# A two-layer encoder trunk on one core: suffix-sum subtractions ahead of head sums, first activations rounded ahead of the second weight slot, and the next layer's first x tiles transposed between the last banks

## The reference

```python
for layer in range(2):
    h = rms_norm(x, norm1_g[layer])
    proj = h @ w_in[layer]              # q, k, v of three mixers and the gate logits
    ya = diff_attention(...)            # two softmax maps a head, partial rotary on q and k
    yb = chunk_band_attention(...)
    yc = stick_breaking_attention(...)  # log_keep = log_sigmoid(-z) below the diagonal;
                                        # later = suffix sum of log_keep over the keys
                                        # a = exp(log_sigmoid(z) + later)
    x = x + (sum of sigmoid(gate_i) * (y_i @ P_i)) @ w_out[layer]
    h2 = rms_norm(x, norm2_g[layer])
    x = x + peer(h2, ...)               # 16384 experts, top-16 a head, weights u and v
```

## Time and profile before

| | |
|---|---|
| median of 3 runs | 2221.88 us (2221.85 to 2223.79) |
| the profiled execution, its own time | 2224.01 us |
| its span, first to last instruction | 2222.3 us |
| PE busy | 2184.6 us, 98% of the span |
| DVE busy | 1591.6 us, 72% |
| ACT busy | 1197.9 us, 54% |
| POOL busy | 570.6 us, 26% |
| mean granted clock of PE | 0.996 |

### The profile page before, as it was taken

How to read it: one execution, slowest core, us unless ns; L and a number is a source line. 1 busy time by engine, 2 the same in 40 slices (tenths; PEclk the granted TensorE clock), 3 DMA queues, 4 the chain that set the end, 5 groups by cost and what they waited for, 6 DMA issues and landing times.

```text
span 2222.3 us, 41570 instructions
## 1 busy us (share of the span) xinstructions
PE 2184.6 (98%) x14116; PEld 1968.4 (89%) x14116; DVE 1591.6 (72%) x2784; ACT 1197.9 (54%) x1936; POOL 570.6 (26%) x286
## 2 busy tenths in 40 slices
PE   8999999999999999999999999999999999999999
PEld 6789999999999988888877899999899999888887
DVE  5667858978897556666657678599788975566665
ACT  5755545478885343333367554454788854333332
POOL 1300006876662000000013000178666610000000
PEclk9999999999999999999999999999999999999999
DMA  6444554544444556566654445445444445556564
GB/s 223 143 142 137 178 187 144 180 161 150 146 149 146 188 186 191 193 192 190 197 187 147 139 147 194 157 160 184 153 151 147 147 152 188 189 190 194 196 193 152
DMA packets 103761, 377.24 MB, mean 170 GB/s; under 512 B 11760, under 2 KB 11760, under 8 KB 103152
## 3 DMA queue, kind: packets, MB, share of 16 engines
q1 hardware_dynamic: 102528, 371.24, 51.0%
q10 hardware_dynamic: 1136, 4.79, 0.6%
HBM read 374.94 MB, written 1.05 MB: 169 GB/s over the span
## 4 chain that ended last, share of the span: by engine, by line
PE 94%; DVE 3%; ACT 2%; issue 1%; DMA 0%; SPq 0%; ACTq 0%; DVEq 0%
PE ps L489 29%; PE ps L490 28%; PE ps L491 28%; PE ps L806 3%; PE ps L498 1%; DVE w_lo L1252 1%; PE ps L616 1%; PE ps L775 1%; ACT w_hi L924 1%; PE ps L577 0%; DMA raw<-in_stream 0%; PE ps L589 0%; PE ps L687 0%; DVE arena L1353 0%; ACT hot L1172 0%
## 5 line engine op out<-in xcount | busy, mean ns | idle before, releaser
L1107 ACT ACTIVATE w_hi<-raw 128x1024 fp32r<-128x1024 f32 x512 | 521.4, 1055 | 510.1 <-PE ps L491 509.9
L489 PE MATMUL ps<-hT_hi,w_hi 128*128 128x256 f32 x2688 | 770.5, 287 | 5.1 <-DVE arena L1670 5.1
L490 PE MATMUL ps<-hT_lo,w_hi 128*128 128x256 f32 x2688 | 762.6, 284 | 0.0
L491 PE MATMUL ps<-hT_hi,w_lo 128*128 128x256 f32 x2688 | 762.4, 284 | 0.0
L474 POOL TENSOR_TENSOR w_lo<-raw,w_hi 128x1024 fp32r<-128x1024 f32 x208 | 498.8, 2407 | 272.5 <-ACT w_hi L1107 272.5
L489 PEld LDWEIGHTS ps<-hT_hi,w_hi 128*128 128x128 f32 x2688 | 517.7, 193 | 10.6 <-issue 7.8
L490 PEld LDWEIGHTS ps<-hT_lo,w_hi 128*128 128x128 f32 x2688 | 517.9, 193 | 0.9
L491 PEld LDWEIGHTS ps<-hT_hi,w_lo 128*128 128x128 f32 x2688 | 517.5, 193 | 0.0
L1637 DVE TENSOR_TENSOR w_lo<-raw,w_hi 128x1024 fp32r<-128x1024 f32 x304 | 358.2, 1220 | 91.2 <-ACT w_hi L1107 91.2
L489 PE MATMUL ps<-w_hi,wgt_hi 128*128 128x512 f32 x1024 | 398.9, 390 | 0.5 <-DVE wgt_lo L1732 0.5
L490 PE MATMUL ps<-w_lo,wgt_hi 128*128 128x512 f32 x1024 | 398.6, 389 | 0.0
(11 more groups left out here) (194 smaller groups left out, 2515.5 us busy)
## 6 DMA issues: line engine op xcount, KB each, us to landing
raw<-in_w_u SPq DMA_DIRECT2D x256, 512.0 KB, 3.3
raw<-in_w_v SPq DMA_DIRECT2D x256, 512.0 KB, 3.8
raw<-in_stream SPq DMA_DIRECT2D x192, 512.0 KB, 3.3
arena<-in_bias ACTq DMA_DIRECT2D x2, 1024.0 KB, 5.8
arena<-in_subk ACTq DMA_DIRECT2D x2, 1024.0 KB, 6.4
x<-in_x SPq DMA_DIRECT2D x4, 256.0 KB, 5.6
out<-x SPq DMA_DIRECT2D x4, 256.0 KB, 2.0
arena<-in_params ACTq DMA_DIRECT2D x2, 283.5 KB, 6.3
```

What stands on the lines that cost most here:

```text
L489: mm(out_, left[0], right[0], start=start, stop=False, skip_group_check=group)
L490: mm(out_, left[0], right[1], start=False, stop=False, skip_group_check=group)
L491: return mm(out_, left[1], right[0], start=False, stop=stop, skip_group_check=group)
L1107: f(w_hi[:, slot, :], raw[:, slot, :], ACT.Copy).then_inc(hi_ready.sem, 1)
```

## The change

Four edits. On DVE, `c_take_later(0)` goes from after slot 22 to after slot 20 and `c_take_later(1)` from after slot 23 to after slot 21, and `head_block(2)` from after slot 20 to after slot 21, behind `c_take_later(1)`. On ACT, `round_tiles(0, (0, 1))` goes between `split(0)` and `split(1)`, and `load_small()` behind `split(1)`. On PE, tiles 0 and 1 of x are transposed before the layer loop (for layer 0) and after groups 1 and 2 of the last product (for the next layer; the loop does this in the last layer too); tile 2 stays at the head of the layer and tile 3 goes behind slot 0. On DVE, tiles 0 and 1 of the next layer are multiplied by the gain and their rests written between the last additions to x, and its slot 0 moves one addition ahead; the order of tiles 2 and 3 follows PE's.

```diff
+            norm_transposes(x_there, (0, 1))
             with pe.Fori(0, LAYERS) as layer:
...
-                norm_transposes(lambda n: pe.wait_ge(x_ready[n].sem, x_ready[n].at(layer, 16)), range(4))
+                norm_transposes(x_done, (2,))
...
+                        if 4 * cb + k == 0:
+                            norm_transposes(x_done, (3,))
...
                     last.then_inc((v_part if n < 3 else v_mm).sem, 1)
+                    if n in (1, 2):
+                        norm_transposes(x_next, (n - 1,))
...
+                split(0)
+                round_tiles(0, (0, 1))
+                split(1)
                 load_small()
-                split(0)
-                split(1)
-                round_tiles(0, (0, 1))
...
-                gain_tiles(0, (0, 1))
                 if layer == 0:
+                    gain_tiles(0, (0, 1))
                     split((0,))
-                rest_tiles(0, (0, 1))
+                    rest_tiles(0, (0, 1))
+                gain_tiles(0, (2,))
                 split((1,))
-                gain_tiles(0, (2, 3))
+                gain_tiles(0, (3,))
                 split((2,))
                 rest_tiles(0, (2, 3))
...
-                    19: ((c_sums, 1), (head_norm, 3)), 20: ((c_keep, 1), (head_block, 2)),
-                    22: ((c_take_later, 0), (head_norm, 4)), 23: ((c_take_later, 1), (head_norm, 5)),
+                    19: ((c_sums, 1), (head_norm, 3)), 20: ((c_keep, 1), (c_take_later, 0)),
+                    21: ((c_take_later, 1), (head_block, 2)), 22: ((head_norm, 4),), 23: ((head_norm, 5),),
...
-                    if n == 1 and layer + 1 < LAYERS:
-                        split((0,), layer + 1)
+                    if layer + 1 < LAYERS:
+                        if n == 0:
+                            split((0,), layer + 1)
+                        if n == 1:
+                            gain_tiles(0, (0,), layer + 1)
+                        if n == 2:
+                            rest_tiles(0, (0,), layer + 1)
+                            gain_tiles(0, (1,), layer + 1)
+                            rest_tiles(0, (1,), layer + 1)
```

More of the change, by code:

```diff
@@ L499, in transposes, with norm_transposes, x_there, x_done @@
                 return last
+            def norm_transposes(done, tiles):
+                for n in tiles:
+                    done(n)
+                    transposes(ps[:, n, :], x_tile(n), 4).then_inc(normT_mm.sem, 1)
+            def x_there(n):
+                pe.wait_ge(x_ready[n].sem, 16)
+            norm_transposes(x_there, (0, 1))
             with pe.Fori(0, LAYERS) as layer:
[L502 to L506, removed]
+                def x_done(n):
+                    pe.wait_ge(x_ready[n].sem, x_ready[n].at(layer, 16))
+                def x_next(n):
+                    pe.wait_ge(x_ready[n].sem, x_ready[n].at(layer, 32))
                 def spread(which):
@@ L1253, in split, with gain_tiles @@
                                         w_hi[:, i % SLOTS, :].bitcast(F), ALU.subtract).then_inc(w_ready.sem, 1)
-                def gain_tiles(which, tiles):
+                def gain_tiles(which, tiles, layer=layer):
                     for n in tiles:
@@ L1263, in gain_tiles, with rest_tiles @@
                                         gain.unsqueeze(2).broadcast_to([P, 4, P]), ALU.mult).then_inc(gained.sem, 1)
-                def rest_tiles(at, tiles):
+                def rest_tiles(at, tiles, layer=layer):
                     for n in tiles:
```

## The result

The changed kernel is slower: 2227.82 us, the median of 15 runs (2226.82 to 2230.05), against 2222.84 (2221.33 to 2227.07, 15 runs) for the kernel before, a ratio of 1.0021 with a 95% interval of 1.0014 to 1.0028. That is 5.0 us more, where the prediction had 0.9 less, and it is outside the range. The profiled execution has a span of 2226.4 us in place of 2222.3, so 4.1 us more to explain, and by page part 1 most of it is idle or slow time and not work: PE is busy for 2.5 us more, with eight more matmuls than before, which take 0.98 us at the pace of the earlier trace rows, and idle for 1.6 more.

The account below looks back on a forecast made before the run. PE, busy 98% of the span, was taken as the bound, with 9.0 us of waits as ceiling of direct gains. Terms -1.4 + 0 + 1.0 - 0.5 + 0 = -0.9 took 2221.88 to 2221.0 us, range 2216.8 to 2223.4.

Parts of the forecast that it names:

- the start of layer 1: From loop's turn to spread(0): slot 0 starts 1.35 us sooner, but the diagonal comes when it came; 0, bounds -0.7 to +0.5.
- The clock, term 0: Behind the suffix sums' idle: one slow matmul stretch in two layers, as before; 0 us, ends -1.6 and +1.6.
- Start of layer 0, -1.4: PE begins slot 0 at 10.45, takes the diagonal at 24.91 where spread(0) ran at 26.34: -1.4 us.
- The rests and the diagonal of layer 1: At layer 1's start the rests are ready, and PE waits up to 0.9 us for the diagonal before spread(0): 0.
- Last layer, +1.0: Two tiles' unused transposes between the last product's groups delay the last addition and store: +1.0 us, between 0.8 and 1.2.
- Suffix sums, -0.25 a layer: Piece 2's wait of 2.33 us becomes about 2.1 at piece 4: -0.25 us a layer, -0.5 in both.
- case 2: In the suffix sums POOL's powers aren't held and ACT is next: -1.06 us a layer, 2219.4 us; chance 0.15.
- case 5: In the suffix sums POOL's powers take longest, holding back piece 4: +2.2 a layer, 2225.9 us, 2227.5 with slow stretch; chance 0.04.

Follow-up runs that it names:

- The late wait alone: Kernel before plus one PE wait, ahead of group 3 of the last product, for the addition to x tile 1: 2227.44 us, ratio 1.0014.
- the loop written out: Changed kernel with PE's loop over the layers written out, nothing else changed: 2219.61 us, ratio 0.9982 to the kernel before.
- tile 0 alone ahead: Changed kernel with only tile 0 transposed between the last groups, tile 1 back at the layer's head: 2225.38 us, ratio 1.0011 to the kernel before.
- The suffix sums alone: Kernel before with only the change's new DVE order of the suffix sums: 2225.86 us, ratio 1.001.
- the start alone: Kernel before with only ACT's new order at the start and tile 3's transposes behind slot 0 in both layers: 2223.78 us, ratio 1.0001.
- the wait for tile 0: Kernel before plus one PE wait, ahead of group 3 of the last product, for the addition to x tile 0: 2221.98 us, ratio 0.9997.
- start and suffix sums: Changed kernel without its layer-boundary edit, so no transposes between the last groups: 2224.68 us, ratio 1.0006 to the kernel before.

## Why the prediction was wrong

**The failed step** as to the mechanism is in the start of layer 1; the clock, further down, is the other and costs more. It reads: "The loop's turn took 1.08 us from the last matmul's slot to 1117.66 and I see nothing that shortens it", with half a microsecond more as the upper bound. I took the idle time that the trace shows for the turn's cost. It was what stuck out from under the matmuls still queued. The change puts a wait on PE that ends at 1112.37 with one group behind it, and then 3.06 us stick out: 2.1 more. The late wait alone shows it (3.4 us, +1.7 to 2.4 at equal clock), and the loop written out shows the reverse (no idle time, 8.2 us less, though some 2 of them have nothing to do with the turn). With 2.1 more the prediction would have been 2223.1, still in its range; the clock took it out. The prediction asks what a step of DVE or POOL is queued behind, but didn't ask it of PE's own instruction stream at the new wait. The Trainium skill ("Perfetto Trace Analysis", section "Sequencer Loop") says that a sequencer pushes instructions for its engine into a queue and runs control instructions itself. The traces agree, in that the turn left 0.3 to 1.0 us idle where nothing held PE's instructions late, 1.5 with tile 0 alone ahead, and 3.1 to 3.5 where the wait for tile 1 did.

**The clock, term 0.** Its ends were -1.6 and +1.6, for one stretch. The profiled execution has three new ones at or behind places that bind (1117, 1209, 1803) and has lost one (96): two more, 3.2 us. The bound failed since it looked at one place only. Of the three, that at 1117 follows the idle time of the turn; that at 1803 can't be put down to the change. Idle of 2.2 us at piece 4, with eight transposes behind it, was priced as if it were the idle at piece 2. The suffix sums alone lower the mean clock as much as the whole change; why piece 4 is the worse place is not shown.

**Start of layer 0, -1.4:** right, -1.67 at the spread. Two misses in the working partly cancel: PE began 0.43 us sooner than predicted, and slot 0 took 5.10 us (10.02 to 15.12) in place of 4.87. But the start alone shows that this isn't 1.6 us of the run: 2223.78 against 2222.94. At equal clock it is 0.1 to 0.9 less. A gain in the list of milestones is spent again when the slow stretches fall otherwise.

**The rests and the diagonal of layer 1:** right in kind. The tile's rest was ready (1116.35), PE waits 0.69 for the diagonal as in layer 0 (about 0.9 predicted), and without the turn and the slow stretch the spread would have come 0.2 sooner than the sum had it.

**Last layer, +1.0:** right, +0.92.

**Suffix sums, -0.25 a layer:** right, the waits are 2.15 and 2.17 at piece 4. POOL's powers took 2.75 us in layer 1 and in layer 0, between the 1.64 and the 3.87 of the earlier trace rows; they were held, so case 2 fell, and case 5 with it. One of them:

```profile
1199.68 2.75 POOL L444 TENSOR_TENSOR qk_rs<-qk_rs,half_neg 128x8 f32<-128x8 f32 x1
```

**The sum again,** for the profiled execution with the turn as measured: -1.67 - 0.2 (rests and diagonal) - 0.3 (suffix sums) + 2.14 + 0.92 = +0.9, and +3.2 for two slow stretches, 4.1 us: the span's difference. None of the five cases had the turn in it, and the one on the other side named POOL; a time above 2226.3 had been given 0.03, all of it to that case.

## What to carry to other kernels

An idle time at a loop's turn is what the queued work leaves uncovered, and not its cost: before a wait is added near the end of a loop's body, count the work behind it on that engine against 5 us here, or write the loop out. Moving a wait to another piece gained nothing here; interleaving the steps so that neither piece waits gained 3.9 us. In a kernel that is 98% busy on one engine, idle of 2 us and more can cost again through the clock, so a change is judged by the mean clock of many runs and not by milestones alone.

## What the runs showed of the hardware

From the end of a late wait to PE's first instruction of the next pass it was 5.17, 5.37, 5.38 and 5.24 us in four kernels, with the weight load beside it or without. With a wait that ended 1.36 us sooner it was 4.15. I can't explain both with one constant.

The DMA packets of the traces give a part of it. The profile has a queue q8 of instruction loads, in pieces of 16 KB; in the changed kernel, the whole span and then the window from 1115.00 to 1116.25:

```profile
q8 instruction: 50, 0.82, 0.2%
```

```profile
q8 instruction: 1, 0.02, 4.8%
```

That piece started at 1115.06 and took 0.96 us, and PE went on 1.52 us behind its end. In all eleven kernels with the loop, one or two such pieces start ahead of the next pass, and PE's first instruction of it comes 1.52 to 2.19 us after the last one's end; in the kernel before and the changed one with the loop written out there is none from 1104 to 1124. With the wait for tile 1 the last piece took 1.98 us, with the wait for tile 0 it took 0.94: that is 1.04 of the 1.22 us between 5.37 and 4.15. So the turn seems to contain a load of instructions. This is argued from the times; the profile doesn't say which engine these pieces are for, and no run changed them.

In two kernels without a late wait the turn's idle time was 0.31 us with the start alone and 1.02 with start and suffix sums. The last such piece ended at 1113.22 and 1113.33 in them and PE went on 1.52 us later in both; what differs is when the last group ran out, at 1114.43 and 1113.83.

The slow stretches in the body of these traces take 1.7 us by (1 - clock) x length, or twice that. After 3.06, 3.44 and 3.46 us of idle at the turn the clock fell each time, after 1.5 or less at the turn never. After the 2.2 to 2.3 us in the suffix sums it fell in some layers and not in others, and so it did after the 2.57 us near 1802.
